# Products with the values in quarter-array tiles over two PSUM banks, probabilities scaled on ScalarE, and a new order of the attention steps

## The chip, the cores and the metric

The kernel runs on one core of a Trainium2 chip. The metric is the device time of one execution in microseconds (us), the median of several runs; less is better. The engines named below are TensorE (PE; PEld is its weight load), VectorE (DVE), ScalarE (ACT), GpSimd (POOL) and SyncE (SP).

## What is computed

The reference is one decoder layer over 512 positions of width 1024. A sliding-window attention and a Mamba-2 mixer (SSD) run side by side and are merged by gates; a gated MLP follows. The change touches only the attention, which is this:

```
qb = q.reshape(Bsz, nb, W, N_KV_HEADS, G, HEAD_DIM)
...
scores = jnp.einsum('bnqhgd,bnshd->bnhgqs', qb, kb).astype(jnp.float32) * (HEAD_DIM ** -0.5)
...
valid = (dist >= 0)[None] & (dist < WINDOW)[None] & (kpos >= 0)
...
m = jnp.maximum(scores.max(axis=-1), sink)
p = jnp.where(valid, jnp.exp(scores - m[..., None]), 0.0)
denom = p.sum(axis=-1) + jnp.exp(sink - m)
probs = (p / denom[..., None]).astype(v.dtype)
out = jnp.einsum('bnhgqs,bnshd->bnqhgd', probs, vb)
```

There are 4 blocks of 128 positions, 4 key/value heads with 4 query heads each, and head size 64. A query sees its own block up to itself, and of the block before it the keys behind its own place there: of the two triangles each fills half of a 128x128 square.

## The kernel before

Every projection is a product of float32 numbers split into a rounded part (`_hi`) and a rest (`_lo`); `three` issues three matmuls for each of 8 slices of the width. A tile of 128 output features is a **unit**: 24 matmuls of 128x512 on TensorE. Two units make a **chunk**, for which the weights are loaded (SyncE), rounded (ScalarE, `w_hi`, L576) and subtracted (VectorE, `w_lo`, L856) one chunk ahead. Chunks 3 to 6 (units 6 to 13) are the queries, 7 to 10 (units 14 to 21) `bc`, 11 and 12 `xs`, 13 and 14 `z`, 15 and 16 `xs`, 17 and 18 `z`. A unit of `bc` or `xs` also has a causal convolution: ScalarE starts `conv_acc` from the unit's bank (L772), VectorE adds three taps from the same bank (L1207), ScalarE takes tanh (L776) and VectorE makes the output (L1212). Even units use bank 0 and odd ones bank 1, so a unit can start only when VectorE has done the third tap of the unit two before it (semaphore `conv_tap`). A unit of `z` needs only a tanh and one VectorE operation.

Attention rides on these units. It has 16 **steps** n, one for each key/value head and block; `att_step(n)` gives head and block, and steps 2i and 2i+1 are a **pair**: two heads of the same block. Of the eight pairs two (steps 0 and 1, 8 and 9) are of the first block and have no block before them. A step runs through these stages:

- TensorE `scores` (for both steps of a pair, L1305 and L1311) into banks 2 to 5; ScalarE `own_scores` copies the own block (L608); VectorE `mask_and_max` masks the block before, takes the maximum and prepares the bias (L931 to L939).
- ScalarE `exponentials`, with the sums of the rows (L614, L617); VectorE `probabilities`: denominator, reciprocal and the scaling of 128x512 probabilities (L944, L946, L948).
- TensorE `probs_t` transposes four heads' probabilities into bank 6 (L1321); VectorE `probs_t_masked` copies them out under the two masks (L956, L958).
- TensorE `values`, once a pair, multiplies them by the values into bank 7 (L1331); ScalarE `attended_hi` rounds the result (L623) and VectorE `attended_lo` takes the rest (L967).

Nothing is scheduled at run time: each engine works its own list in order and waits on semaphores. The place of a stage in the lists comes from two tables. `ATT_AT[n]` is the start of step n in units, counted from unit 14, and `ATT_STAGES` adds to it a number of slots for each engine and stage. TensorE has two slots in a unit (slot 0 after its first half, slot 1 at its end). ScalarE and VectorE have three: before they start on the unit's result, after `conv_acc` or the taps, and at the end. `SSD_STAGES` does the same for the Mamba-2 steps from unit 38 on. `take(bank, semaphore, value)` makes TensorE wait for the last reader of a bank before it writes it, and notes who will read it next.

## Time and profile before

| | |
|---|---|
| Time, median of 3 runs | 1030.68 us (1030.05 to 1030.86) |
| Time of the profiled execution | 1030.5 us |
| Its span | 1028.8 us |
| TensorE busy | 1019.6 us, 99% |
| VectorE busy | 642.0 us, 62% |
| ScalarE busy | 457.5 us, 44% |
| GpSimd busy | 69.4 us, 7% |
| Granted TensorE clock | full in all slices |

The span is from the first to the last record of the trace; the execution's own time is 1.7 us longer. Busy shares are over the whole span, in which stages with different limits follow one another. Matmuls are pipelined and their records overlap, so the distance from one start to the next says more than a record's length.

### The profile page before, as it was taken

To read this page: it belongs to the slowest core of one execution; us is meant where nothing else is said; L and a number is where in the kernel's file an instruction comes from. 1 tells how busy PE (TensorE), PEld (TensorE's weight loads), DVE (VectorE), ACT (ScalarE), POOL (GpSimd) and SP (SyncE) were. 2 spreads that over 40 slices of the span, in tenths; PEclk is the share of its full clock that TensorE was granted. 3 is DMA by queue.
4 is the path that set the end of the run, shared out by engine and by line. 5 is a ranking of instruction groups with operands and counts; after the bars stand their busy time and mean duration, and the time that the engine had idled before them with its cause. 6 is when DMAs were issued, how large, how long until landed. Compare 5 with 4: busy or idle time off the path is not lost.

```text
span 1028.8 us, 13393 instructions
## 1 busy us (share of the span) xinstructions
PE 1019.6 (99%) x5095; PEld 832.2 (81%) x5095; DVE 642.0 (62%) x909; ACT 457.5 (44%) x818; POOL 69.4 (7%) x112
## 2 busy tenths in 40 slices
PE   9999999999999999999999999999999999999997
PEld 8887777777788888888888888898888888888886
DVE  7636999794476685985754544666666676641323
ACT  6344555454555545765533222544444444331233
POOL 0000000000231120122220100000000000000000
PEclk9999999999999999999999999999999999999999
DMA  7622221225556424445362743223232223332322
GB/s 219 123 85 82 83 62 63 83 83 120 159 133 162 133 72 137 140 127 153 100 205 82 266 143 108 77 82 113 91 122 82 82 85 119 93 128 87 95 69 82
DMA packets 123498, 116.48 MB, mean 113 GB/s; under 512 B 21342, under 2 KB 111782, under 8 KB 123447
## 3 DMA queue, kind: packets, MB, share of 16 engines
q1 hardware_dynamic: 95509, 94.74, 29.9%
q10 hardware_dynamic: 25346, 12.59, 5.2%
q0 software_dynamic: 2592, 8.46, 2.2%
q8 instruction: 34, 0.56, 0.2%
q14 instruction: 17, 0.14, 0.0%
HBM read 109.41 MB, written 6.36 MB: 113 GB/s over the span
## 4 chain that ended last, share of the span: by engine, by line
PE 89%; DVE 8%; ACT 2%; issue 1%; DMA 0%; SPq 0%; ACTq 0%; DVEq 0%
PE banks L1259 27%; PE banks L1260 27%; PE banks L1261 27%; DVE conv_acc L1207 3%; PE banks L1363 1%; DVE w_lo L856 1%; PE banks L1356 1%; PE banks L1331 1%; PE banks L1351 1%; PE banks L1339 1%; DMA w_raw<-in_w_in 0%; ACT probs L614 0%; PE banks L1321 0%; PE banks L1311 0%; ACT w_hi L576 0%
## 5 line engine op out<-in xcount | busy, mean ns | idle before, releaser
L856 DVE TENSOR_TENSOR w_lo<-w_raw,w_hi 128x1024 fp32r<-128x1024 f32 (+1 forms) x166 | 198.3, 1234 | 123.7 <-ACT w_hi L576 122.4
L576 ACT ACTIVATE w_hi<-w_raw 128x1024 fp32r<-128x1024 f32 (+1 forms) x166 | 164.1, 1037 | 109.2 <-PE banks L1261 107.9
L1259 PE MATMUL banks<-xn_hi,w_hi 128*128 128x512 f32 x528 | 211.5, 401 | 0.0
L1260 PE MATMUL banks<-xn_lo,w_hi 128*128 128x512 f32 x528 | 206.1, 390 | 0.0
L1261 PE MATMUL banks<-xn_hi,w_lo 128*128 128x512 f32 x528 | 206.0, 390 | 0.0
L1259 PE MATMUL banks<-hn_hi,w_hi 128*128 128x512 f32 (+1 forms) x376 | 141.3, 376 | 0.0
L1260 PE MATMUL banks<-hn_lo,w_hi 128*128 128x512 f32 (+1 forms) x376 | 141.2, 375 | 0.0
L1261 PE MATMUL banks<-hn_hi,w_lo 128*128 128x512 f32 (+1 forms) x376 | 141.2, 375 | 0.0
L1259 PEld LDWEIGHTS banks<-xn_hi,w_hi 128*128 128x128 f32 x528 | 99.1, 188 | 28.2 <-issue 8.5
L1261 PEld LDWEIGHTS banks<-xn_hi,w_lo 128*128 128x128 f32 x528 | 99.1, 188 | 21.4
L1260 PEld LDWEIGHTS banks<-xn_lo,w_hi 128*128 128x128 f32 x528 | 99.3, 188 | 19.0
L1261 PEld LDWEIGHTS banks<-hn_hi,w_lo 128*128 128x128 f32 x376 | 70.8, 188 | 12.9
L1259 PEld LDWEIGHTS banks<-hn_hi,w_hi 128*128 128x128 f32 x376 | 70.8, 188 | 12.8
L1260 PEld LDWEIGHTS banks<-hn_lo,w_hi 128*128 128x128 f32 x376 | 70.8, 188 | 12.6
L1259 PE MATMUL banks<-w_hi,act_hi 128*128 128x512 f32 x176 | 68.5, 389 | 0.0
L1260 PE MATMUL banks<-w_lo,act_hi 128*128 128x512 f32 x176 | 68.5, 389 | 0.0
L1261 PE MATMUL banks<-w_hi,act_lo 128*128 128x512 f32 x176 | 68.5, 389 | 0.0
L1207 DVE SCALAR_TENSOR_TENSOR conv_acc<-banks,half_conv,conv_acc 128x511 f32<-128x511 f32 (+2 forms) x72 | 53.8, 747 | 4.8 <-ACT conv_acc L772 3.0
L1259 PE MATMUL banks<-y_hi,w_hi 128*128 128x512 f32 x128 | 50.0, 391 | 0.0
L1261 PE MATMUL banks<-y_hi,w_lo 128*128 128x512 f32 x128 | 49.8, 389 | 0.0
L1260 PE MATMUL banks<-y_lo,w_hi 128*128 128x512 f32 x128 | 49.8, 389 | 0.0
L1028 DVE SCALAR_TENSOR_TENSOR conv_acc<-banks,param_cols,conv_acc 128x511 f32<-128x511 f32 (+1 forms) x44 | 32.9, 748 | 23.2 <-ACT conv_acc L693 20.3
(221 smaller groups left out, 1429.8 us busy)
## 6 DMA issues: line engine op xcount, KB each, us to landing
w_raw<-in_w_in SPq DMA_DIRECT2D x29, 1024.0 KB, 5.4
w_raw<-in_w_up SPq DMA_DIRECT2D x22, 1024.0 KB, 5.0
decay<-acs_scratch ACTq DMA_DIRECT2D x16, 512.0 KB, 5.9
w_raw<-in_w_ssd_o SPq DMA_DIRECT2D x8, 1024.0 KB, 5.3
w_raw<-in_w_down SPq DMA_DIRECT2D x8, 1024.0 KB, 5.0
w_raw<-in_w_in SPq DMA_DIRECT2D x16, 256.0 KB, 4.5
w_raw<-in_w_attn_o SPq DMA_DIRECT2D x16, 256.0 KB, 4.7
decay_off<-acs_scratch ACTq DMA_DIRECT2D x32, 128.0 KB, 3.6
```

What stands on the lines that cost most here:

```text
L576: A.activation(whi[:, c % 2, lo_:hi_], raw[:, c % 2, lo_:hi_], ACT.Copy).then_inc(w_rounded, 1)
L856: V.tensor_tensor(wlo[:, c % 2, lo_:hi_], raw[:, c % 2, lo_:hi_], f32(whi[:, c % 2, lo_:hi_]), ALU.subtract).then_inc(w_split, 1)
L1028: V.scalar_tensor_tensor(out=acc[:, back:SEQ], in0=PS[:, 2 * j + u, 0:SEQ - back], scalar=FW(2 - back, j, 2 * it + u), in1=acc[:, back:SEQ ...
L1207: V.scalar_tensor_tensor(out=acc[:, back:SEQ], in0=b[:, 0:SEQ - back], scalar=CW(3 - back, t), in1=acc[:, back:SEQ], op0=ALU.mult, op1=ALU ...
L1259: T.matmul(out_, w[0], m[0], start=first, stop=False)
L1260: T.matmul(out_, w[0], m[1], start=False, stop=False)
L1261: return T.matmul(out_, w[1], m[0], start=False, stop=last)
L1331: ins = T.matmul(PS[rows, 7, :], v[:, b_ - back, (g + hh) * HD:(g + hh + 1) * HD], probs.rearrange("p j q -> p (j q)"), start=back == 1 or ...
L1339: ins = T.transpose(PS[:, 2, t * P:(t + 1) * P], xs[:, TG * g + t, tok], ident[:, :])
L1351: T.matmul(PS[:, 6, :], bncb[:, 0:P], xcd[:, :], start=True, stop=True)
L1356: T.matmul(PS[:, 4, t * P:(t + 1) * P], st[:, t * P:(t + 1) * P], bc[:, NG + g, tok], start=True, stop=True)
L1363: ins = T.matmul(PS[o:o + HD, 5, (hd // 2) * P:(hd // 2 + 1) * P], xc[:, hd * HD:(hd + 1) * HD], ag[:, n % 3, hd, :], start=True, stop=True)
```

## The change

The values' products are cut into halves of keys and of queries. `part(keys, queries, back, start, stop)` issues two matmuls, one for each head of the pair, with 64 keys, 64 output features and 4 x 64 query columns. Early keys go to bank 2 and late ones to bank 7. Three quarters of each square are computed; the quarter that the mask leaves empty is skipped (in the first block it is computed once, so that bank 7 is filled). ScalarE copies bank 2 into the new tile `attended` (`attended_left`), VectorE adds bank 7 to it (`attended_sum`), and `attended_hi` and `attended_lo` read that tile and no bank. VectorE no longer scales the probabilities: its stage is now called `denominators`, and ScalarE has a stage `probabilities` with four activations of 128x128. The two tables change: transposes and values are one TensorE slot (half a unit) later in a step, and the steps from 3 on start 0.25 or 0.5 units earlier.

```diff
 ATT_STAGES = (
-    ("PE", "scores", 1), ("PE", "probs_t", 5), ("PE", "values", 7), ("ACT", "own_scores", 1),
-    ("ACT", "exponentials", 4), ("ACT", "attended_hi", 10),
-    ("DVE", "mask_and_max", 1), ("DVE", "probabilities", 4), ("DVE", "probs_t_masked", 7),
-    ("DVE", "attended_lo", 10))
+    ("PE", "scores", 1), ("PE", "probs_t", 6), ("PE", "values", 8), ("ACT", "own_scores", 1),
+    ("ACT", "exponentials", 4), ("ACT", "probabilities", 5), ("ACT", "attended_left", 11), ("ACT", "attended_hi", 12),
+    ("DVE", "mask_and_max", 1), ("DVE", "denominators", 4), ("DVE", "probs_t_masked", 8),
+    ("DVE", "attended_sum", 11), ("DVE", "attended_lo", 12))
...
-ATT_AT = (-4.5, -3.25, -2, -0.5, 1, 2.75, 4.5, 6.25, 8, 9.75, 11.5, 13, 14.25, 15.5, 16.75, 18)
+ATT_AT = (-4.5, -3.25, -2, -0.75, 0.75, 2.5, 4.25, 6, 7.75, 9.25, 11, 12.5, 13.75, 15, 16.25, 17.5)
...
+        if _n == 0 and _w == "load_decay":
+            _v = -6
...
+        att = sb("attended", [P, 2, GQ, HD], 136)
...
+                    elif what == "attended_left":
+                        if n % 2:
+                            eng.wait_ge(a_pv, n // 2 + 1)
+                            A.activation(att[:, :, :, :].rearrange("p h j q -> p (h j q)"), PS[:, 2, :],
+                                         ACT.Copy).then_inc(a_left, 1)
+                    elif what == "probabilities":
+                        eng.wait_ge(a_rd, n + 1)
+                        for j in range(GQ):
+                            ins = A.activation(Pr[:, n % 2, j, :], Pr[:, n % 2, j, :], ACT.Identity,
+                                               scale=rden[:, n % 2, j:j + 1])
+                        ins.then_inc(a_pr, 1)
...
-                        eng.wait_ge(a_pv, n // 2 + 1)
...
+                        eng.wait_ge(a_sum, n // 2 + 1)
...
-                        eng.wait_ge(a_rd, n + 1)
-                        V.tensor_tensor(Pr[:, k, :, :], Pr[:, k, :, :], bcast(rden[:, k, :], GQ, P),
-                                        ALU.mult).then_inc(a_pr, 1)
...
+                    elif what == "attended_sum":
+                        if n % 2:
+                            eng.wait_ge(a_left, n // 2 + 1)
+                            av = att[:, :, :, :].rearrange("p h j q -> p (h j q)")
+                            V.tensor_tensor(av, av, PS[:, 7, :], ALU.add).then_inc(a_sum, 1)
...
-                        take(7, a_ol, n // 2 + 1)
-                        for back in (1, 0) if b_ else (0,):
+                        take(2, a_left, n // 2 + 1)
+                        take(7, a_sum, n // 2 + 1)
+
+                        def part(keys, queries, back, start, stop):
+
                             for hh in range(2):
-                                rows = slice(hh * HD, (hh + 1) * HD)
-                                probs = ptp_of[hh][:, :, :] if back else ptc[:, hh, :, :]
-                                ins = T.matmul(PS[rows, 7, :], v[:, b_ - back, (g + hh) * HD:(g + hh + 1) * HD],
-                                               probs.rearrange("p j q -> p (j q)"), start=back == 1 or b_ == 0,
-                                               stop=back == 0)
+                                ks, qs = slice(keys * HD, keys * HD + HD), slice(queries * HD, queries * HD + HD)
+                                probs = ptp_of[hh][ks, :, qs] if back else ptc[ks, hh, :, qs]
+                                ins = T.matmul(PS[hh * HD:(hh + 1) * HD, (2, 7)[keys],
+                                                  queries * GQ * HD:(queries + 1) * GQ * HD]
+                                               .rearrange("p (j q) -> p j q", j=GQ),
+                                               v[ks, b_ - back, (g + hh) * HD:(g + hh + 1) * HD],
+                                               probs, start=start, stop=stop)
+                            return ins
+
+                        if b_:
+                            part(0, 0, 1, True, False)
+                            part(1, 1, 1, True, False)
+                            part(0, 0, 0, False, True)
+                            part(1, 1, 0, False, True)
+                            part(0, 1, 0, True, True)
+                            ins = part(1, 0, 1, True, True)
+                        else:
+                            part(0, 0, 0, True, True)
+                            part(1, 1, 0, True, True)
+                            part(0, 1, 0, True, True)
+                            ins = part(1, 0, 0, True, True)
```

What these tables move is seen in the engines' lists. Line numbers of the changed kernel differ: L1259 to L1261 are now L1277 to L1279, L1331 is L1352, L576 is L580, L772 is L787, L776 is L791.

**TensorE**, near unit 30. `probs_t_prev` with two numbers is the block before for the two heads of the pair, `v` the values. Before:

```order
L1261 MATMUL banks<-xn_hi,w_lo 128x512
L1331 MATMUL banks<-probs_t_prev_86,v 64x512
L1331 MATMUL banks<-probs_t_prev_87,v 64x512
L1331 MATMUL banks<-probs_t_cur,v 64x512 x2
L1321 MATMUL banks<-ident,probs 128x128 x4
```

And in the changed kernel, for the values of steps 10 and 11:

```order
L1279 MATMUL banks<-xn_hi,w_lo 128x512
L1352 MATMUL banks<-probs_t_prev_87,v 64x256
L1352 MATMUL banks<-probs_t_prev_88,v 64x256
L1352 MATMUL banks<-probs_t_prev_87,v 64x256
L1352 MATMUL banks<-probs_t_prev_88,v 64x256
L1352 MATMUL banks<-probs_t_cur,v 64x256 x6
L1352 MATMUL banks<-probs_t_prev_87,v 64x256
L1352 MATMUL banks<-probs_t_prev_88,v 64x256
L1339 MATMUL banks<-ident,probs 128x128 x4
L1329 MATMUL banks<-kT,qT 64x192 x16
```

Four matmuls with 512 columns have become twelve with 256, and the scores of steps 14 and 15, which write bank 2 again, now stand in the same place behind values and transposes.

**ScalarE**, from the tanh of unit 19 to the tanh of unit 20. `w_hi` is the rounding of the weights of chunk 11. Before:

```order
L776 ACTIVATE conv_tanh<-conv_acc 128x512
L614 ACTIVATE probs,small<-scores,small 128x128 x4
L617 ACTIVATE small<-small 128x4
L576 ACTIVATE w_hi<-w_raw 128x1024 x2
L623 ACTIVATE a_hi<-banks 128x4x128
L772 ACTIVATE conv_acc<-banks,half_conv 128x512
L608 ACTIVATE scores<-banks 128x512
L776 ACTIVATE conv_tanh<-conv_acc 128x512
```

And in the changed kernel:

```order
L791 ACTIVATE conv_tanh<-conv_acc 128x512
L630 ACTIVATE probs<-probs,small 128x128 x4
L580 ACTIVATE w_hi<-w_raw 128x1024 x2
L625 ACTIVATE attended<-banks 128x512
L787 ACTIVATE conv_acc<-banks,half_conv 128x512
L638 ACTIVATE a_hi<-attended 128x2x4x64
L612 ACTIVATE scores<-banks 128x512
L791 ACTIVATE conv_tanh<-conv_acc 128x512
```

The exponentials of step 6 moved ahead of the tanh of unit 19, and the scaling of its probabilities stands between that tanh and the rounding of the weights; the copy of bank 2 stands ahead of `conv_acc` of unit 20.

**VectorE**, from the outputs of unit 21 (`bc`) to those of unit 22 (`xs`). `small` holds denominators and maxima, `neg_tile` marks step 8, which is of the first block. Before:

```order
L944 TENSOR_TENSOR small<-small 128x4
L946 RECIPROCAL small<-small 128x4
L948 TENSOR_TENSOR probs<-probs,small 128x512
L1212 SCALAR_TENSOR_TENSOR bc<-conv_tanh,conv_acc 128x512
L856 TENSOR_TENSOR w_lo<-w_raw,w_hi 128x1024 x2
L1207 SCALAR_TENSOR_TENSOR conv_acc<-banks,half_conv,conv_acc 128x511
L1207 SCALAR_TENSOR_TENSOR conv_acc<-banks,half_conv,conv_acc 128x510
L1207 SCALAR_TENSOR_TENSOR conv_acc<-banks,half_conv,conv_acc 128x509
L956 TENSOR_TENSOR probs_t_prev_87<-banks,mask_prev_t 128x512
L958 TENSOR_TENSOR probs_t_cur<-banks,tri 128x512
L931 COPY_PREDICATED scores<-mask_prev,neg_tile 128x512
```

And in the changed kernel:

```order
L959 TENSOR_TENSOR small<-small 128x4
L961 RECIPROCAL small<-small 128x4
L1230 SCALAR_TENSOR_TENSOR bc<-conv_tanh,conv_acc 128x512
L871 TENSOR_TENSOR w_lo<-w_raw,w_hi 128x1024 x2
L946 COPY_PREDICATED scores<-mask_prev,neg_tile 128x512
L949 TENSOR_REDUCE small<-scores 128x4
L951 TENSOR_TENSOR small<-small 128x4
L953 TENSOR_SCALAR small<-small 128x4
L954 TENSOR_TENSOR small<-small 128x4
L1225 SCALAR_TENSOR_TENSOR conv_acc<-banks,half_conv,conv_acc 128x511
L1225 SCALAR_TENSOR_TENSOR conv_acc<-banks,half_conv,conv_acc 128x510
L1225 SCALAR_TENSOR_TENSOR conv_acc<-banks,half_conv,conv_acc 128x509
```

The scaling is gone, and the block of the maximum of step 8, which stood behind the taps of unit 22, stands ahead of them.

## Rows read from the trace of the kernel before

**Rows 1.** Busy time by stage, 115 to 180 us; columns: stretch, its length, engines.
```profile
115.00:180.00 65.00, 64.21 (x368) 49.08 (x368) 58.84 (x103) 35.52 (x90) 0.00 (x0) 1.00 0.21 66
```

**Rows 2.** Chain of waits; columns: start us, length us, what.
```profile
121.03 1.53 ACT probs L614 x8
123.17 0.69 DVE probs L948
```

**Rows 3.** Timeline of TensorE around the values of the third pair.
```profile
131.31 0.39 PE L1261 MATMUL banks<-xn_hi,w_lo 128*128 128x512 f32 x1
131.63 1.08 PE L1331 MATMUL banks<-probs_t_prev,v 128*64 128x512 f32 x4
...
133.50 0.50 PE L1259 MATMUL banks<-xn_hi,w_hi 128*128 128x512 f32 x1
```

**Rows 4.** Timeline of TensorE around scores with two blocks of keys.
```profile
124.50 1.53 PE L1311 MATMUL banks<-kT,qT 64*64 64x192 f32 x32
125.96 0.50 PE L1259 MATMUL banks<-xn_hi,w_hi 128*128 128x512 f32 x1
```

**Rows 5.** Timeline of TensorE at two waits for VectorE.
```profile
147.51 0.39 PE L1261 MATMUL banks<-xn_hi,w_lo 128*128 128x512 f32 x1
148.27 0.66 PE L1321 MATMUL banks<-ident,probs 128*128 128x128 f32 x4 [0.37 <-DVE probs L948]
148.86 1.10 PE L1311 MATMUL banks<-kT,qT 64*64 64x64 f32 x32
149.89 0.50 PE L1259 MATMUL banks<-xn_hi,w_hi 128*128 128x512 f32 x1
...
179.00 0.39 PE L1261 MATMUL banks<-xn_hi,w_lo 128*128 128x512 f32 x1
179.81 1.08 PE L1331 MATMUL banks<-probs_t_cur,v 128*64 128x512 f32 x4 [0.42 <-DVE probs_t_cur L958]
180.82 0.50 PE L1259 MATMUL banks<-xn_hi,w_hi 128*128 128x512 f32 x1
```

**Rows 6.** Timeline of VectorE; in brackets idle time before the row.
```profile
116.14 2.32 DVE L1207 SCALAR_TENSOR_TENSOR conv_acc<-banks,half_conv,conv_acc 128x511 f32<-128x511 f32 x3
...
127.39 0.73 DVE L931 COPY_PREDICATED scores<-mask_prev,banks 128x512 f32<-128x512 int32 x1
...
129.23 0.68 DVE L956 TENSOR_TENSOR probs_t_prev<-banks,mask_prev_t 128x512 f32<-128x512 f32 x1
...
130.43 2.31 DVE L1207 SCALAR_TENSOR_TENSOR conv_acc<-banks,half_conv,conv_acc 128x511 f32<-128x511 f32 x3
...
135.14 0.16 DVE L944 TENSOR_TENSOR small<-small 128x4 f32<-128x4 f32 x1 [1.01 <-ACT small L617]
...
147.13 0.15 DVE L944 TENSOR_TENSOR small<-small 128x4 f32<-128x4 f32 x1
...
147.53 0.69 DVE L948 TENSOR_TENSOR probs<-probs,small 128x512 f32<-128x512 f32 x1
148.14 0.68 DVE L1212 SCALAR_TENSOR_TENSOR bc<-conv_tanh,conv_acc 128x512 f32<-128x512 f32 x1
148.86 2.36 DVE L856 TENSOR_TENSOR w_lo<-w_raw,w_hi 128x1024 fp32r<-128x1024 f32 x2
151.13 2.31 DVE L1207 SCALAR_TENSOR_TENSOR conv_acc<-banks,half_conv,conv_acc 128x511 f32<-128x511 f32 x3
```

**Rows 7.** Timeline of ScalarE, in attention and behind it.
```profile
147.24 0.63 ACT L776 ACTIVATE conv_tanh<-conv_acc 128x512 f32<-128x512 f32 x1 [2.34 <-DVE conv_acc L1207]
147.78 1.99 ACT L576 ACTIVATE w_hi<-w_raw 128x1024 fp32r<-128x1024 f32 x2
149.68 0.76 ACT L772 ACTIVATE conv_acc<-banks,half_conv 128x512 f32<-128x512 f32 x1
...
245.86 1.28 ACT L645 ACTIVATE decay<-decay,small 128x128 f32<-128x128 f32 x4
250.76 0.60 ACT L783 ACTIVATE conv_tanh<-banks 128x512 f32<-128x512 f32 x1 [3.62 <-PE banks L1261]
```

12 lines of the change are left out of this document (7 added, 5 removed).

## The prediction, made before the changed kernel ran

> **What bounds the kernel now.** I read the stages first. Attention runs from 60 to 240 us of the span, beside the projections. In its middle, 115 to 180 us, TensorE is busy for 64.21 of 65 us and VectorE for 58.84; ScalarE has 35.52 [rows 1]. So TensorE bounds the time, with VectorE just behind it. The chain of waits agrees: there it runs over ScalarE's exponentials and VectorE's scaling, and not over TensorE [rows 2]. Away from this stretch it runs nearly everywhere over TensorE. What shortens TensorE's own work shortens the kernel, if VectorE delivers.
>
> I call a tile of projections (24 matmuls) a unit. From the second half of unit 20 (133.50) to the last matmul of unit 22 (147.51) lie 59 matmul steps, one group of transposes (0.44) and 0.10 after the values [rows 3, 5]: 13.47 / 59 = 0.228 us a step, 5.48 us a unit.
>
> **TensorE's work.** Now the values of a pair of heads take 131.63 to 133.50, 1.87 us: eight records of 128*64 tiles, two heads side by side, each product in two passes [rows 3]. A pass streams 512 columns; four in a row make about 1.71 us and 0.16 stays for start and end. The first block has no keys before it: 1.01 us (179.81 to 180.82) [rows 5].
>
> No row shows the new form, 64*64 tiles with 256 columns. The nearest are the scores, which run in such tiles with different banks for the two row halves, exactly as here: 32 passes of 192 columns take 1.46 us (124.50 to 125.96), and 32 of which half have 128 and half 64 take 1.03 (148.86 to 149.89) [rows 4, 5]. With a pass at 512 columns worth 0.427, 192 columns are 0.160, and 32 passes over four tiles 1.28: 0.18 is left. For the second, the tiles with 128 columns need 8 x 0.107 = 0.85, and again 0.18 is left. So four tiles overlap fully, and the longest one counts. The new form has 24 passes of 0.213: 6 x 0.213 + 0.18 = 1.46 us. First block: 4 x 0.213 + 0.18 = 1.03. Six pairs have a block before them, two have none: 6 x (1.46 - 1.87) + 2 x 0.02 = **-2.4 us**. Bounds: the two rows above leave hardly 0.1 a pair (0.6 in all); without any overlap of the row halves it is a rival below.
>
> **Waits that go.** TensorE waits for VectorE's scaling before the transposes at 148.27: the gap from 147.51 is 0.76 instead of 0.23. It waits for masked probabilities at 179.81: 0.81 instead of the 0.32 that rows 3 show [rows 3, 5]. Transposes half a unit (2.7 us) later, and the masking of that pair now ahead of the rounding of weights on VectorE, take both away: 0.53 + 0.49 = **-1.0 us**. Bounds: 0 and -1.2 (there is a smaller wait of this kind near 124 us).
>
> **What VectorE and ScalarE get.** VectorE loses 16 scalings, which hold it for 0.61 each (147.53 to 148.14) and gains 8 sums, priced by the same form at 0.6 [rows 6]: 16 x 0.61 - 8 x 0.6 = 5 us less. ScalarE gains 16 groups of four scalings. The nearest row is the decay's activation of 128x128 with a column operand: four in 1.28 us [rows 7]; the next instruction can start after about 1.2. It also gains 8 copies out of a bank, at most 0.6 each. That is 24 us more on an engine with much idle time. As a sum this costs nothing; as an order it does, since both sit in a loop: VectorE's taps, ScalarE's tanh, what is queued behind it, then the weights' rounding or the next unit's start, then VectorE again.
>
> The Trainium skill, TensorEngine Tiling (Array Packing), Performance Considerations, speaks against this change: tiling speeds up TensorE but not the reading of its banks, and the copy may become the bottleneck. By it the second bank's copy and sum would eat the gain; the sum below finds that the copy costs little and ScalarE's scalings the most. No row here decides it.
>
> **The new wait.** I follow VectorE from the taps of unit 17, which start at 116.14 [rows 6] and which nothing ahead moves by more than some 0.2, to the taps of unit 22, which free the bank for unit 24. Prices as the distance to the next row where they overlap: taps 2.23 (2.31 busy, of which 0.08 overlaps), output 0.60, block of maximum 1.84, masking 1.20, denominators 0.40, rounding rest of two half chunks 2.27 [rows 6]. The changed order has there 6 taps (13.4), 3 maskings (3.6), 5 outputs (3.0), 3 denominators (1.2), 3 roundings (6.8), 3 blocks of maximum (5.5; now there are two, the third stands behind these taps), one sum and one rest of attention (1.2): 34.7 us.
>
> VectorE's idle time for ScalarE is added, with tanh 0.54, w_hi 1.90 (half of it 0.95), conv_acc 0.7 [rows 7], exponentials 1.63 (rows 2 show 1.53 for the chain's part):
> - unit 17: tanh and exponentials (2.2) against masking and output (1.8): 0.4; then the first half of w_hi against the denominators: 0.55
> - unit 18: w_hi, the scaling and conv_acc (1.9 + 1.2 + 0.7 = 3.8) against 3.2 of VectorE: 0.6
> - units 19 and 21: after the taps ScalarE does tanh, now the scaling, then half of w_hi (0.6 + 1.2 + 1.0 = 2.8), VectorE only denominators and output (1.0): 1.8, twice.
>
> That is 5.2 us. Today the longest one there is 1.01 [rows 6]. With 0.4 of small gaps the taps of unit 22 end at 116.14 + 34.7 + 5.2 + 0.4 = 156.4.
>
> TensorE arrives at unit 24 as follows. Unit 22 ends today at 147.51 + 0.23 = 147.74, without its wait. Two values before it save 0.82, a wait 0.17, and the scores that stand behind unit 22 now stand inside it (+1.23 with their gaps): 147.9. Unit 23 with its transposes adds 5.92: 153.8. So TensorE waits 156.4 - 153.8 = **+2.6 us**. The pair's values stand behind this point now and ahead of it before, so nothing of the wait is made good there. In the next units VectorE has spare time again (a TensorE stop gives it that), and the z units, in which it has no taps to do, have room.
>
> **Small terms.** In unit 30 the changed order puts values, transposes and scores in one place, and the scores want bank 2, which ScalarE copies out only after the values: 0.1 to start, 0.6 for the copy, minus 0.4 of transposes between: **+0.3**. Four places in place of three have scores right behind transposes, which costs 0.05 each, and one place fewer has values before them: **+0.1**. The load of the first decay goes behind two roundings of weights: its four activations, now at 245.86, start some 2 us later, into the 3.62 us in which ScalarE idles before 250.76 [rows 7]; cost nothing, up to 1 us if that idle time were gone. The new `take(2, ...)` ahead of the values waits for a maximum block that is a unit older; nothing. No queue of SyncE or GpSimd moves.
>
> **Sum.** -2.4 - 1.0 + 2.6 + 0.3 + 0.1 = -0.4 on the profiled execution's 1030.5, which is 0.2 under the median of the runs: 1030.1 by the one, 1030.3 by the other. The wait of 2.6 is the softest term, and a TensorE unit that comes a little late shortens it: I shade it to 2.3, **1030.0 us**. A change within 0.2% (2.1 us, about what a measurement of this kernel can tell from none) is the likeliest, 1028.6 to 1032.7.
>
> **Rivals.**
> 1. The wait at unit 24 doesn't come, because VectorE, 5 us lighter, reaches unit 17 early or ScalarE's scalings fall into its idle time: -2.4 - 1.0 + 0.4 = 1027.5 to the median's scale. For it: ScalarE is busy only 55% of the stretch [rows 1]. Against it: the two scalings of units 19 and 21 stand exactly where VectorE has nothing else. Half of the wait gives 1028.8, so the wait must be under 1.2 us to pass the bound. Chance 0.38 for faster by over 0.2%.
> 2. Slower: the loop binds in each of the five unit pairs from 14 to 24, and not in two. Each pair adds 1.2 to 1.8 of idle time (the scaling ahead of w_hi); three more make 3.6 to 5.4, and VectorE's lag grows by that less what it saves (2 us). Then the waits are 2.6 + 2 to 3.4 and the time 1032 to 1033.5. It decides from a total wait of 5 us on. Chance 0.13.
> 3. The change doesn't do what it says: the row halves don't run side by side. Then 24 passes over two tiles take 12 x 0.213 + 0.18 = 2.74 us, +0.87 for six pairs and +0.86 for two, 7 us more work, of which the wait at unit 24 hides some: 1034 to 1037. The scores' rows are against it. Chance 0.04.
>
> **Range.** Forecast 0.45, faster 0.38, slower 0.17. From rival 1's full gain to the start of rival 2's loss: 1027.4 to 1032.5. Own range of the forecast: 1028.7 to 1031.5.
>
> **What would show it.** Values at 1.4 to 1.5 us from first matmul to the next projection, in four-tile form; over 1.7 would sink the first term. No wait before the transposes near 147 or the values near 179. A gap before the first projection of unit 24, near 154, released by VectorE's taps (`conv_acc`), with `w_lo` starting over 1 us after the output before it, and w_hi behind a scaling on ScalarE. A gap of 0.3 before scores near 205. If TensorE's gap near 154 is missing, the prediction is wrong on the fast side; if such gaps stand before several units, on the slow side. No difference is expected after 245 us.

## The result, and the profile after

The median of 20 runs is 1032.57 us (1030.43 to 1034.8); the kernel before has 1030.53 (1030.03 to 1031.35, 20 runs). The ratio is 1.0019, 95% interval 1.0013 to 1.0025: slower by about 0.2%. I had forecast 1030.0 and a range to 1032.5, which the median just misses. The difference is small but clear of the noise, and it goes the other way than I forecast. Two things in these numbers need explaining. The profiled execution is one of the quick ones, 1030.94 us, 1.6 us below the median of its own kernel. And the runs lie 4.4 us apart, those of before 1.3.

The profiled execution first. The values' products in the changed kernel's timeline of TensorE (start, length, engine, line, operation, tiles, count; in brackets the idle time ahead and its releaser):

```profile
133.26 0.39 PE L1279 MATMUL banks<-xn_hi,w_lo 128*128 128x512 f32 x1
133.58 0.66 PE L1352 MATMUL banks<-probs_t_prev,v 64*64 64x256 f32 x8
...
134.72 0.38 PE L1352 MATMUL banks<-probs_t_prev,v 64*64 64x256 f32 x2
135.04 0.50 PE L1277 MATMUL banks<-xn_hi,w_hi 128*128 128x512 f32 x1
```

From 133.58 to 135.04 are 1.46 us, where [rows 3] had 1.87. Four tiles run side by side, as the first term had it. The waits at the transposes near 147 and the values near 179 [rows 5] are gone; the waits of TensorE between 150 and 240 us are one row (waited for in all, times, longest):

```profile
PE banks L1277 <- DVE conv_acc L1225: 3.4, 2, 2.7
```

The two are these. At unit 24, on TensorE:

```profile
153.76 0.39 PE L1279 MATMUL banks<-xn_hi,w_lo 128*128 128x512 f32 x1
156.87 0.50 PE L1277 MATMUL banks<-xn_hi,w_hi 128*128 128x512 f32 x1 [2.72 <-DVE conv_acc L1225]
```

The step is 3.11 us in place of 0.23, a stop of 2.88. How VectorE came to be late is seen two units earlier, first ScalarE and then VectorE:

```profile
133.11 0.63 ACT L791 ACTIVATE conv_tanh<-conv_acc 128x512 f32<-128x512 f32 x1 [2.34 <-DVE conv_acc L1225]
133.65 1.26 ACT L630 ACTIVATE probs<-probs,small 128x128 f32<-128x128 f32 x4
134.82 2.00 ACT L580 ACTIVATE w_hi<-w_raw 128x1024 fp32r<-128x1024 f32 x2
```

```profile
133.78 0.69 DVE L1230 SCALAR_TENSOR_TENSOR bc<-conv_tanh,conv_acc 128x512 f32<-128x512 f32 x1 [0.42 <-ACT conv_tanh L791]
135.89 2.36 DVE L871 TENSOR_TENSOR w_lo<-w_raw,w_hi 128x1024 fp32r<-128x1024 f32 x2 [1.43 <-ACT w_hi L580]
```

The scaling stands between tanh and `w_hi` for 1.17 us, and VectorE, with nothing else to do, waits 1.43. The same happens at 150.36.

The second wait, at unit 34, is in no term of the sum:

```profile
231.58 0.60 PE L1339 MATMUL banks<-ident,probs 128*128 128x128 f32 x4
232.83 0.50 PE L1277 MATMUL banks<-xn_hi,w_hi 128*128 128x512 f32 x1 [0.65 <-DVE conv_acc L1225]
```

TensorE goes on 1.25 us after transposes that take 0.35 from their start to the next one's (231.62 to 231.97 in the kernel before): 0.9 lost. ScalarE and then VectorE before it:

```profile
227.65 0.62 ACT L638 ACTIVATE a_hi<-attended 128x512 fp32r<-128x512 f32 x1
228.47 1.28 ACT L630 ACTIVATE probs<-probs,small 128x128 f32<-128x128 f32 x4 [0.20 <-DVE small L961]
229.66 0.77 ACT L787 ACTIVATE conv_acc<-banks,half_conv 128x512 f32<-128x512 f32 x1
```

```profile
228.35 0.66 DVE L984 TENSOR_TENSOR a_lo<-attended,a_hi 128x512 fp32r<-128x512 f32 x1
230.46 2.32 DVE L1225 SCALAR_TENSOR_TENSOR conv_acc<-banks,half_conv,conv_acc 128x511 f32<-128x511 f32 x3 [1.44 <-ACT conv_acc L787]
```

Here the scaling stands ahead of `conv_acc`, and VectorE's taps wait for that. The stretches, to be read beside [rows 1] (length, then busy time and instructions of PE, PEld, DVE, ACT, POOL, the granted clock, DMA share, GB/s):

```profile
115.00:180.00 65.00, 62.28 (x393) 48.60 (x392) 56.12 (x100) 42.02 (x111) 0.00 (x0) 1.00 0.21 66
180.00:240.00 60.00, 59.22 (x384) 45.84 (x382) 45.81 (x85) 36.85 (x103) 0.00 (x0) 1.00 0.25 77
```

TensorE was idle for 0.79 us of the first stretch and is for 2.72 now, with both other engines far from full: two engines wait for each other in turn, and neither is the bound by its load.

To compare executions I use TensorE's own marks, from the row of a line's matmuls (count, least/median/longest ns, first and last start): the first projection with `xn_hi` and the first with `a_hi`. Between them lies all of the attention. Before, and after:

```profile
L1259 PE MATMUL banks<-xn_hi,w_hi x528: 389/389/504, 26.3 to 526.4; 128*128 128x512 f32 x176
L1259 PE MATMUL banks<-a_hi,w_hi x64: 389/389/504, 262.2 to 363.2; 128*128 128x512 f32 x64
```

```profile
L1277 PE MATMUL banks<-xn_hi,w_hi x528: 389/389/504, 26.2 to 526.9; 128*128 128x512 f32 x176
L1277 PE MATMUL banks<-a_hi,w_hi x64: 389/389/504, 262.7 to 363.7; 128*128 128x512 f32 x64
```

I call the distance of the first starts the attention stretch: 235.9 us before, 236.5 after. It leaves out what differs from run to run at the start (the mark itself lies between 25.5 and 27.3 us in the 15 traces of the study) and later on. From the first `y_hi` matmul (528.4 in this trace) to the last of the gated MLP every trace has 494.1 or 494.2 us.

### The profile page after: what moved, and what is told of

It is laid out like the page before. It is cut to its first block, busy times and chain, and to the rows that moved or that the text cites. A ratio compares the mean times of both kernels' runs of the same rounds, so it can differ in the third digit from the quotient of the medians.

```text
span 1029.2 us, 13697 instructions
## 1 busy us (share of the span) xinstructions
PE 1017.7 (99%) x5215; PEld 835.0 (81%) x5215; DVE 636.1 (62%) x901; ACT 480.4 (47%) x890; POOL 70.1 (7%) x112
## 4 chain that ended last, share of the span: by engine, by line
PE 91%; DVE 6%; ACT 2%; issue 1%; DMA 0%; SPq 0%; ACTq 0%; DVEq 0%
PE banks L1277 28%; PE banks L1279 27%; PE banks L1278 27%; DVE conv_acc L1225 2%; PE banks L1400 1%; DVE w_lo L871 1%; PE banks L1393 1%; PE banks L1388 1%; PE banks L1352 1%; PE banks L1329 1%; PE banks L1376 1%; DMA w_raw<-in_w_in 0%; PE banks L1339 0%; ACT probs L630 0%; PE banks L1288 0%
## 5 line engine op out<-in xcount | busy, mean ns | idle before, releaser
L1277 PE MATMUL banks<-xn_hi,w_hi 128*128 128x512 f32 x528 | 211.7, 401 | 3.4 <-DVE conv_acc L1225 3.4
L580 ACT ACTIVATE w_hi<-w_raw 128x1024 fp32r<-128x1024 f32 (+1 forms) x166 | 164.1, 1037 | 107.6 <-PE banks L1279 107.6
L1279 PE MATMUL banks<-xn_hi,w_lo 128*128 128x512 f32 x528 | 206.0, 390 | 0.0
L1277 PE MATMUL banks<-hn_hi,w_hi 128*128 128x512 f32 (+1 forms) x376 | 141.3, 376 | 0.0
L1279 PE MATMUL banks<-hn_hi,w_lo 128*128 128x512 f32 (+1 forms) x376 | 141.2, 375 | 0.0
L1277 PEld LDWEIGHTS banks<-xn_hi,w_hi 128*128 128x128 f32 x528 | 99.2, 188 | 29.9 <-issue 6.1
L1279 PEld LDWEIGHTS banks<-xn_hi,w_lo 128*128 128x128 f32 x528 | 99.1, 188 | 21.5
L1279 PEld LDWEIGHTS banks<-hn_hi,w_lo 128*128 128x128 f32 x376 | 70.8, 188 | 12.8
L1277 PEld LDWEIGHTS banks<-hn_hi,w_hi 128*128 128x128 f32 x376 | 70.8, 188 | 12.6
L1277 PE MATMUL banks<-w_hi,act_hi 128*128 128x512 f32 x176 | 68.5, 389 | 0.0
L1279 PE MATMUL banks<-w_hi,act_lo 128*128 128x512 f32 x176 | 68.5, 389 | 0.0
L1277 PE MATMUL banks<-y_hi,w_hi 128*128 128x512 f32 x128 | 50.0, 391 | 0.0
L1279 PE MATMUL banks<-y_hi,w_lo 128*128 128x512 f32 x128 | 49.8, 389 | 0.0
```

The costliest lines, as they stand in the source:

```text
L580: A.activation(whi[:, c % 2, lo_:hi_], raw[:, c % 2, lo_:hi_], ACT.Copy).then_inc(w_rounded, 1)
L1277: T.matmul(out_, w[0], m[0], start=first, stop=False)
L1279: return T.matmul(out_, w[1], m[0], start=False, stop=last)
```

## The experiments

Theory A: the stop of nearly 3 us at unit 24 also makes TensorE's granted clock fall in many executions, and that lifts the median over the profiled one. Theory B: the spread has another source. Beside them stands the question of which part of the change makes the wait. Two further theories came up during the study, both on why runs of a kernel differ: theory C, the new form of the values makes them differ; theory D, only a wait at unit 24 does. Medians are of the kernel named; the kernel before had 1030.25 to 1030.56 beside them. Each row is explained below.

| kernel | attention stretch | profiled | median (lowest to highest) |
|---|---|---|---|
| before | 235.9 | 1030.5 | 1030.53 (1030.03 to 1031.35) |
| changed | 236.5 | 1030.94 | 1032.57 (1030.43 to 1034.8) |
| changed again | 236.4 | 1030.48 | 1032.68 (1030.48 to 1033.7) |
| changed, two single executions | 238.0, 238.0 | 1035.27, 1032.63 | |
| step 8's maximum behind the taps | 235.3 | 1029.44 | 1030.24 (1029.44 to 1031.51) |
| scaling on VectorE | 234.0 | 1028.96 | 1029.55 (1028.22 to 1031.22) |
| scaling behind the rounding | 234.8 | 1029.35 | 1029.89 (1028.54 to 1031.69) |
| both places | 234.3 | 1030.17 | 1029.95 (1028.19 to 1031.2) |
| all but the scaling, maximum behind | 233.0 | 1026.74 | 1027.0 (1026.74 to 1028.55) |
| order alone | 234.7 | 1028.8 | 1028.8 (1028.62 to 1029.76) |
| order and scaling | 236.4 | 1031.55 | 1031.09 (1030.34 to 1031.59) |
| before, new values alone | 238.9 | 1033.83 | 1033.7 (1032.94 to 1036.15) |
| before, one stop of 3 us | 239.9 | 1034.49 | 1034.3 (1033.37 to 1035.53) |
| before, stops at z | 240.0 | 1044.6 | 1044.35 (1043.89 to 1044.88) |

### The changed kernel again, three times

> The changed kernel as it is, once more, for a second profiled execution. Theory A (TensorE's granted clock falls after the long stop at unit 24 in most executions): if the profiled one is among the longer runs, 1032 us or more, the stretch right behind the stop, 157 to 162 us, shows matmul steps of 0.43 in place of 0.227 us and a granted clock of about 0.5, worth 1.5 to 3 us, and no other place differs. If it is a quick one near 1030.9 the clock is full there as in the first. Theory B: a long run shows full clock there and the time is lost in several other waits. Median 1032 to 1033 by both.

> The changed kernel again, one profiled execution, to have one of its longer executions (over 1032 us) in a trace. Theory A: behind the stop at unit 24, from 157 us on, matmul steps of 0.43 us and a granted clock near 0.5 for 3 to 5 us. Theory B: full clock there, the time lost in other places.

> As the run before it, a further profiled execution of the changed kernel; the same is expected of it.

The repeat gave a median of 1032.68 and again a quick profiled execution, 1030.48. The two single executions were long ones, 1035.27 and 1032.63. The second of them, TensorE's timeline and windows:

```profile
153.84 0.39 PE L1279 MATMUL banks<-xn_hi,w_lo 128*128 128x512 f32 x1
157.01 0.75 PE L1277 MATMUL banks<-xn_hi,w_hi 128*128 128x512 f32 x1 [2.78 <-DVE conv_acc L1225]
157.56 0.63 PE L1278 MATMUL banks<-xn_lo,w_hi 128*128 128x512 f32 x1
157.98 0.63 PE L1279 MATMUL banks<-xn_hi,w_lo 128*128 128x512 f32 x1
```

```profile
153.80:156.80 3.00, 0.43 (x2) 0.01 (x1) 2.86 (x7) 0.00 (x0) 0.00 (x0) 1.00 0.96 304
157.00:160.00 3.00, 2.99 (x7) 2.41 (x8) 2.19 (x6) 3.00 (x12) 0.00 (x0) 0.51 0.06 20
160.00:164.00 4.00, 4.00 (x34) 2.60 (x34) 3.83 (x8) 3.11 (x8) 0.00 (x0) 0.94 0.00 0
```

The quick execution of the changed kernel, the same window behind the stop:

```profile
157.00:160.00 3.00, 3.00 (x16) 2.23 (x20) 2.32 (x6) 3.00 (x12) 0.00 (x0) 1.00 0.09 27
```

The same stop stands in all four traces (3.11, 3.12, 3.11 and 3.17 from start to start). In two of them the steps behind it are 0.43 us in place of 0.227: half the clock, 1.2 in place of 2.4 GHz, 7 matmul records in place of 16 in three microseconds. Both executions have an attention stretch of 238.0, 1.5 us longer. Of 32 runs of the changed kernel 18 have a mean granted clock of 0.997 or less over the whole program, and their median is 1032.9; the other 14 have 0.998 to 1.0 and 1031.1. (The mean is a rough mark: it takes in the end of the program, where the clock halves too, and the 1035.27 execution has 0.998 although its clock did fall behind the stop. So 18 is rather a lower bound.) Of 80 runs of the kernel before that were taken beside the experiments none has less than 0.998, and none of the 79 runs of the eight kernels below in which TensorE never stops for over 2 us. That a fall follows the stop, and costs 1.5 us, is shown in two traces; that it happens in somewhat over half of the runs is argued from the means, which give 1.8 us between the two groups.

The traces say something on why it comes in one execution and not in the next. In all 15 the clock also falls at the end of the program, where TensorE has nothing more to do. In windows of 0.1 us, the fall lies from 2.4 us (the run with stops at z) to 5.1 us (the order alone) behind the start of the last matmul; the four traces of the changed kernel have 3.4, 3.2, 4.8 and 2.9. So the delay differs from one execution to the next. Behind the last matmul ahead of unit 24 it was 3.4 and 3.3 us in the two long executions, when TensorE had just gone on after 3.1 and 3.2; the two quick ones went on after 3.1 and had no fall. A stop of this length lies within the scatter of the delay.

The first single execution is longer by 2.6 us than the second. Its start is 0.9 later (27.3 against 26.4). It has also waits of ScalarE that the quick execution has not, between 400 and 460 us:

```profile
ACT decay_off L683 <- DMA decay_off<-acs_scratch: 1.7, 1, 1.7
```

A transfer of the Mamba-2 part lands late, and TensorE loses 1.7 us between `a_hi` and `y_hi` (267.4 against 265.7). So B has a share as well: start and late transfers, 2.6 us between these two executions, in which the wait and the fall are the same.

### Step 8's maximum behind the taps of unit 22

```diff
-ATT_AT = (..., 6, 7.75, 9.25, ...)
+ATT_AT = (..., 6, 8, 9.25, ...)
```

> The changed kernel, with step 8's block of maximum (1.86 us on VectorE) behind the taps of unit 22 again and no more ahead of them. In the changed kernel's trace these taps end at 156.8 and TensorE is there at 153.8. Without the block they end near 155.0, so the wait at unit 24 falls from 2.88 to about 1.1 us; the smaller one at unit 34 stays. Theory A (a wait near 3 us on TensorE also makes its granted clock fall for a few microseconds in many executions, and this is what lifts the median of 1032.57 over the profiled execution of 1030.94): the wait gives 1.8 us and the lower clock goes with it, median 1028.8 to 1029.5, runs within 1.5 us of each other. Theory B (the spread of the runs comes from something else in the new order, such as ScalarE's load or the loop of the rounded weights): only the 1.8 us go, median 1030.3 to 1031, the runs still spread over 3 us or more.

The edit puts every stage of step 8 one slot later, on all three engines; the block of the maximum is what leaves VectorE's list ahead of the taps. TensorE at unit 24:

```profile
153.43 0.39 PE L1279 MATMUL banks<-xn_hi,w_lo 128*128 128x512 f32 x1
154.74 0.50 PE L1277 MATMUL banks<-xn_hi,w_hi 128*128 128x512 f32 x1 [0.92 <-DVE conv_acc L1225]
```

The step is 1.31, a wait of 1.08, as expected. The block now delays the masking behind it, and the next values wait 0.60 for that (`PE banks L1352 <- DVE probs_t_cur L970`), so that 1.2 of the 1.8 us are kept. None of 11 runs has a mean clock under 0.998, and the median falls by 2.3, more than the stretch alone, which speaks for A. But A's own forecast missed: 1030.24 is over its 1028.8 to 1029.5 (0.6 of that is the wait before the values) and close to B's 1030.3, and the spread of 2.1 us is not down to 1.5. The median is also 0.8 above the profiled execution, with no fall of the clock in any run; so part of the 1.6 us between the two in the changed kernel has another source than the clock.

### The kernel before, with one stop of 3 us

```diff
                         k_conv += 1
                         take(b, c_tap, 3 * k_conv)
+                        if k_conv == 11:
+                            eng.wait_ge(a_rd, 9)
```

> The kernel before with one wait added: TensorE starts unit 24 only when VectorE has the reciprocals of step 8 (160.46 in its trace), where it now starts at 157.42. All else is as before. It is a stop of TensorE of about 3.0 us, as long as the one that the change makes, without the change. Theory A (the stop also lowers the granted clock in many executions): the time rises by 3 us and by 1 to 2 more in the median, 1034.5 to 1035.5, runs spread over 3 us or more, and the longer runs show the lower mean clock. Theory B: it rises by the stop alone, 1033.0 to 1033.6, with the spread of before, about 1.3 us.

Nothing of the change is in this kernel, and the clock falls here too:

```profile
155.00:160.00 5.00, 2.47 (x11) 0.67 (x9) 4.83 (x11) 3.26 (x12) 0.00 (x0) 1.00 0.15 52
160.90:163.50 2.60, 2.60 (x8) 2.02 (x7) 2.60 (x4) 1.73 (x3) 0.00 (x0) 0.50 0.00 0
163.90:170.00 6.10, 6.10 (x31) 5.01 (x30) 3.15 (x7) 0.78 (x1) 0.00 (x0) 1.00 0.57 175
```

The stretch grows by 4.0 us: 2.9 of stop (156.44 to 160.32, less the 0.95 that the values take there) and 1.6 at half speed (8 steps of 0.43), less the 0.49 wait at the first block's values [rows 5], which is gone because the stop lets VectorE catch up. The median is 3.7 over before (expected 4 to 5 by A, 2.5 to 3 by B), and 4 of 6 runs have 0.997 or less. They spread over 2.2 us, not the 3 expected by A. The stop alone makes the clock fall; the change is needed for it only as the maker of the stop.

### The kernel before, with stops at the units of z

```diff
                         take(b, z_out, k_z)
+                        if k_z > 1:
+                            eng.wait_ge(z_tanh, k_z - 1)
```

> The kernel before with several short stops of TensorE in place of one long one: each unit of z starts only when ScalarE has done the tanh of the unit of z before it, 0.1 + 0.63 us after that unit's end. That is six places (units 27 to 29 and 35 to 37), two or three of them partly covered by scores or transposes: 3 to 4.5 us of idle TensorE in all, none longer than 1 us. Theory A: short stops cost what they last and the granted clock stays full: the time rises by the sum of the gaps, 1033.5 to 1035, and the runs agree within 1.5 us. The rival (it is the amount of idle time in the stretch, not one long stop): as in the kernel with one stop of 3 us, the clock falls behind some of them, 1 to 3 us more and a spread of 3 us.

The median rose by 14 us, not by 3 to 4.5: I had counted 8 units of z, and there are 16; and at one of them ScalarE is far behind. The run still says what it was made for. Windows with two short stops (1.17 and 1.12 us from start to start) inside, then around the one long one (4.47), and behind it; and TensorE's waits:

```profile
172.00:188.00 16.00, 14.49 (x89) 10.33 (x82) 11.08 (x22) 8.82 (x19) 0.00 (x0) 1.00 0.21 67
396.00:402.00 6.00, 2.14 (x10) 1.44 (x8) 3.17 (x5) 5.87 (x7) 0.00 (x0) 0.89 0.28 76
402.20:407.40 5.20, 5.18 (x12) 4.12 (x13) 0.59 (x1) 0.00 (x0) 0.00 (x0) 0.50 0.67 216
```

```profile
PE banks L1259 <- ACT conv_tanh L783: 8.6, 6, 4.1
PE banks L1259 <- issue: 1.8, 3, 0.7
```

The clock stays full behind the short stops and is halved for over 5 us behind the long one. Waits of 10.4 and 2.6 lost at half speed are 13.0 of the 14.1 us by which this execution is longer; the rest I did not trace. The other three runs have mean clocks of 0.998 and the same times, 1043.89 to 1044.88: whether the clock fell in them too stays open.

### The scaling back on VectorE

```diff
-("ACT", "probabilities", 5)
...
                         V.reciprocal(rden[:, k, :], den[:, k, :]).then_inc(a_rd, 1)
+                        eng.wait_ge(a_rd, n + 1)
+                        V.tensor_tensor(Pr[:, k, :, :], Pr[:, k, :, :], bcast(rden[:, k, :], GQ, P),
+                                        ALU.mult).then_inc(a_pr, 1)
```

> The changed kernel with the scaling of the probabilities back on VectorE (one operation of 0.61 us behind the reciprocals) and none on ScalarE; new tables, products with the values and copy of bank 2 stay. Up to the taps of unit 22 VectorE gets three scalings more (1.8 us) and waits less for ScalarE: 1.2 less in units 19 and 21 each, 0.6 in unit 18, 3.0 in all. The wait at unit 24 falls from 2.88 to about 1.7 us, and the one at unit 34 goes (0.8). My prediction's account (ScalarE's scaling ahead of the rounding of weights makes most of VectorE's idle time, and so most of the wait): the profiled execution near 1029.0, and VectorE's idle of 1.43 before w_lo in units 19 and 21 down to about 0.3. The rival (it is the load of VectorE that makes the wait): VectorE later than in the changed kernel, the wait at 24 3.5 us or more, 1031.5 and more. Under theory A (clock falls after a long stop) the median lies close to the profiled execution in the first case.

VectorE has more to do and is earlier. The step at unit 24:

```profile
153.94 0.39 PE L1276 MATMUL banks<-xn_hi,w_lo 128*128 128x512 f32 x1
155.44 0.50 PE L1274 MATMUL banks<-xn_hi,w_hi 128*128 128x512 f32 x1 [1.11 <-DVE conv_acc L1222]
```

1.50 in place of 3.11, and at unit 34 0.76 in place of 1.25: 2.1 us, and the stretch falls by 2.5. `w_lo` at 135.65 and 148.94 starts without any wait that the timeline would show. My account holds, and the rival (VectorE's load) falls; the wait became shorter than I expected (1.27 over the natural step, not 1.7).

### The scaling on ScalarE, behind the rounding of weights

```diff
+        if (_e, _w) == ("ACT", "probabilities") and _s % 6 == 5:
+            _s += 1
```

> The changed kernel with ScalarE's scaling moved behind the rounding of weights wherever it stood right ahead of it; the same work, in another order on ScalarE alone. My account of the wait at unit 24 (the scaling of 1.17 us stands between the tanh and w_hi in units 19 and 21, and VectorE, which has nothing else then, waits for w_hi): VectorE's two idle times of 1.43 us fall to about 0.3, the taps of unit 22 end near 154.5, the wait falls from 2.88 to 0.4 to 0.9 us, profiled 1028.6 to 1029.2, median within 0.6 of that. The rival (ScalarE's load as such holds the loop, wherever the scaling stands; the idle time only moves to another operation): the wait stays above 2 us and the time above 1030.3.

The same work in another order. VectorE:

```profile
133.06 0.69 DVE L1233 SCALAR_TENSOR_TENSOR bc<-conv_tanh,conv_acc 128x512 f32<-128x512 f32 x1 [0.41 <-ACT conv_tanh L794]
134.01 2.36 DVE L874 TENSOR_TENSOR w_lo<-w_raw,w_hi 128x1024 fp32r<-128x1024 f32 x2 [0.25 <-ACT w_hi L583]
```

1.43 became 0.25, twice. The step at unit 24 is 1.68 (152.84 to 154.52), a wait of 1.45 where I expected 0.4 to 0.9: of the 2.4 us that the two places give, VectorE passes on 1.4, since small waits for `conv_acc` (0.31) and the own scores (0.23) take their place. The stretch falls by 1.7. The profiled 1029.35 is a little over the 1028.6 to 1029.2 expected. So the position costs about half of this wait (1.4 of 2.9), and here the load costs something too.

### The parts alone

New values alone, in the order of before, with the scaling on VectorE:

```diff
-("ACT", "attended_hi", 10), ... ("DVE", "attended_lo", 10)
+("ACT", "attended_left", 10), ("ACT", "attended_hi", 11), ... ("DVE", "attended_sum", 10), ("DVE", "attended_lo", 11)
```

> The kernel before with one part of the change: the values' products in quarter-array tiles over banks 2 and 7, with ScalarE's copy, VectorE's sum, and the rounding from the sum. Scaling on VectorE and the order of before stay (the rounding of attention comes a slot later, the load of the first decay too). By the prediction's term: six pairs at 1.46 in place of 1.87 us and two at 1.03, 2.4 us less of TensorE's work. VectorE has 8 sums of 0.6 more; its wait at 148.27 may grow by that (0 to 0.6). Expected 1028.0 to 1028.7 with the spread of before. The rival (the second bank's copy and sum hold TensorE up elsewhere, above all the scores that want bank 2): a wait of 0.5 us or more before scores in several places, and 1029.5 to 1031.

It is 3 us slower where I had expected it about 2 us quicker, by a wait that I had put at 0 to 0.6 us and at one place. TensorE's waits from 115 to 240 us, of this kernel:

```profile
PE banks L1336 <- DVE probs L957: 5.1, 4, 1.7
PE banks L1349 <- DVE probs_t_cur L967: 0.6, 1, 0.6
```

and VectorE ahead of the first of them:

```profile
113.94 0.68 DVE L973 TENSOR_TENSOR attended<-attended,banks 128x512 f32<-128x512 f32 x1
115.31 0.69 DVE L981 TENSOR_TENSOR a_lo<-attended,a_hi 128x512 fp32r<-128x512 f32 x1 [0.70 <-ACT a_hi L632]
```

A pair costs VectorE 1.3 us here and not 0.6: the sum, and a wait for ScalarE's rounding of it, since sum, rounding and rest follow one another at once. In an order in which the transposes wait for VectorE's scaling already [rows 5], that comes out on TensorE at four places before transposes and one before values: from start to start they lose 5.4 us more than before, less the 2.4 of the values, and the stretch is 3.0 longer. The Trainium skill's page TensorEngine Tiling (Array Packing), Performance Considerations, was cited in the prediction for this (emptying the banks may become the bottleneck); in this order the trace agrees.

The new order alone, with the old values and the scaling on VectorE:

```diff
-("PE", "probs_t", 5), ("PE", "values", 7) ... ("DVE", "probs_t_masked", 7)
+("PE", "probs_t", 6), ("PE", "values", 8) ... ("DVE", "probs_t_masked", 8)
...
-ATT_AT = (-4.5, -3.25, -2, -0.5, 1, 2.75, ...)
+ATT_AT = (-4.5, -3.25, -2, -0.75, 0.75, 2.5, ...)
```

> The kernel before with the new order alone: transposes and values half a unit later, steps from 3 on 0.25 or 0.5 units earlier, the masked copies a slot later on VectorE, and the rounding of attention too. Values in their old form (1.87 us), scaling on VectorE, no second bank. The waits before the transposes at 148.27 and the values at 179.81 go: 1.0 us. With the products in the new form and the scaling on VectorE the wait at unit 24 was 1.1 us; here VectorE has no sum (0.6 less) and TensorE arrives 0.8 later (two values), so it is 0 to 0.3. Expected 1029.4 to 1029.9 by my account. The rival (the order by itself makes the wait at unit 24, whatever the rest): 1.5 us or more of wait there and 1031 or more.

The ratio is 0.9986 (0.9977 to 0.9995), and 1028.8 is below the 1029.4 to 1029.9 expected. TensorE has no wait at all between 115 and 240 us, and the stretch is 234.7, 1.2 less. The order does not make the wait.

The order and the scaling on ScalarE, with the old values:

```diff
-("DVE", "probabilities", 4)
+("ACT", "probabilities", 5), ("DVE", "denominators", 4)
```

> The new order with the scaling on ScalarE, and the values in their old form: the change without its first part. Against the run with the order alone the taps of unit 22 come later by what the scaling on VectorE saved in the changed kernel, 2.73 - 1.11 = 1.6 us. There was no wait at unit 24 in that run; I expect 0.8 to 1.4 us now and 0.4 at unit 34, 1029.8 to 1030.6 by my account. By the rival (without the sum VectorE has the room, the scaling on ScalarE costs nothing): 1028.8. On the spread: theory C (the new form of the values makes runs differ) expects 1.3 us or less; theory D (the wait at unit 24 does) more, if the wait is over 1 us.

The steps are 1.30 at unit 24 and 0.85 at unit 34: waits of 1.07 and 0.5, in the bounds expected, and the stretch is 1.7 longer than with the order alone. The time of 1031.09 is half a microsecond over what I gave. With the new order, the scaling on ScalarE brings the wait without the new values. These make it longer by 1.8 us: counted from the first projection, TensorE comes to unit 24 0.7 earlier and VectorE's taps end 1.1 later (0.6 of it the sum). So the new values, with the scaling on ScalarE, gain nothing: the stretch is 236.4 without them and 236.5 with them.

### Without the wait

The changed kernel with the scaling on VectorE and step 8's maximum behind the taps, the edits of two runs above together:

> The changed kernel with both causes of the wait at unit 24 taken away: the scaling on VectorE, and step 8's block of maximum behind the taps of unit 22. In the run with the scaling on VectorE alone the wait was 1.11 us; the block is 1.86, so it goes. Left are the new form of the values (2.4 us less) and the new order (the waits of 1.0 us gone), with 0.3 to 0.4 before the scores near 204 and as much at unit 34. Expected 1027.5 to 1028.2, the quickest so far. On the spread: the kernels with the new form of the values have so far spread over 2 to 4 us, those without it (before, and the order alone) over 1.2. Theory C (the new form of the values itself makes runs differ): 2 us or more here too. Theory D (runs differ only where TensorE waits for VectorE at unit 24 for more than about 1 us): within 1.3 us, as no such wait is left.

1027.0 us, ratio 0.9970 (0.9957 to 0.9982), quicker than both kernels and than the 1027.5 to 1028.2 expected. TensorE's waits that are left between 115 and 240 us:

```profile
PE banks L1349 <- DVE probs_t_cur L967: 0.2, 1, 0.2
PE banks L1274 <- DVE conv_acc L1222: 0.2, 1, 0.2
```

```profile
115.00:180.00 65.00, 64.80 (x415) 50.63 (x414) 62.64 (x112) 38.40 (x96) 0.00 (x0) 1.00 0.23 72
```

VectorE is busy for 62.64 of 65 us, more than in any kernel here, and TensorE for 64.80. The new values are in, and five of six runs lie within 0.32 us, the sixth 1.5 above: a spread of 1.8, between the 1.3 that theory D expects and the 2 or more of theory C (the new values make runs differ). Six runs don't decide it. The table speaks rather for C: the six kernels with the new values and no long stop spread over 1.8 to 3.2 us, the two with the old ones and no long stop over 1.1 and 1.3, as the kernel before. How the new values would do that no run shows.

All three parts, with both places set:

```diff
-ATT_AT = (..., 6, 7.75, 9.25, ...)
+ATT_AT = (..., 6, 8, 9.25, ...)
...
+        if (_e, _w) == ("ACT", "probabilities") and _s % 6 == 5:
+            _s += 1
```

> The changed kernel with all its parts, and two stages placed otherwise: ScalarE's scaling behind the rounding of weights where it stood ahead of it, and step 8's block of maximum behind the taps of unit 22. With the first alone the step at unit 24 was 1.68 us where 0.23 is natural; the block is 1.86, so the wait goes. If the waits and what the clock loses behind the long one are the whole of the difference, the profiled execution is 1029.35 - 1.45 + 0.2 (the wait before the next values, as in the kernel with the scaling on VectorE) = 1028.1, and the runs show no mean clock under 0.998; against the kernel with the scaling on VectorE (1026.7) it has 0.5 more at unit 34. If ScalarE's scaling costs by itself, a wait of 1 us or more is left in units 17 to 26 and the time stays above 1029.

No wait is left at unit 24, and no run has a mean clock under 0.998. But the stretch is 234.3 against 233.0 with the scaling on VectorE: TensorE waits 0.5 before values, 0.2 before transposes and 0.9 at unit 34 (0.6 in its row of waits). The two places explain 2.2 of the 3.5 us by which the changed kernel's stretch exceeds the shortest one; 1.3 is left to the scaling on ScalarE, of which 0.5 is a matter of place again: at unit 34 it still stands ahead of `conv_acc` (0.9 lost in place of 0.4). The profiled execution missed my 1028.1 by 2.1: its start is 0.8 later than in the run from which I had reckoned, late transfers take 0.5 more, and the stretch fell by 0.5 where I had 1.25. Its runs spread over 3 us without any wait at unit 24, so theory D (runs differ only by that wait) falls.

## Why the prediction was wrong

- **Values, -2.4**: right. 1.46 and 1.03 us in the traces, and from the order alone to the order with new values and the maximum behind the taps the stretch falls by 1.7, near the 1.5 that 2.4 less 0.3 at unit 30, 0.4 at unit 34 and 0.2 before values would make.
- **Waits that go, -1.0**: right. The order alone gives 1.2.
- **The new wait, +2.6, shaded to 2.3**: its place, its releaser and its makers were right; it measured 2.88. VectorE's idle time for ScalarE, 5.2 us by the sum, is 5.24 in the rows; what was missing is that the taps of unit 17 start 0.38 later than taken (116.52). Shading it was wrong: 0.6 lacks in the forecast by it.
- **The step that failed** is the pricing of this wait by its length. A stop of TensorE of that length costs another 1.5 us in the executions in which the granted clock falls behind it, and by the mean clocks these are at least 18 of 32. The forecast of 1030.0 is to be set against 1031.1, the median of the runs whose mean clock shows no fall; against all runs the forecast lacks 2.6. Of this, 1.1 stand against the runs without a fall and come from the shaded wait (0.6) and the one at unit 34 (0.9); the other 1.5 are the clock. Without the clock the change would have been no gain either: its sign hangs on the two waits, its size on the clock.
- **"The z units have room"**: wrong. At unit 34 the scaling stands ahead of `conv_acc` of unit 32 and costs TensorE 0.9. I had followed VectorE from unit 17 to unit 24 only, and the changed order puts scalings before `conv_acc` later on too. This is the second step that failed, a term that the sum has at nothing.
- **Unit 30, +0.3**: right, 0.79 from the transposes to the scores. Load of the decay, 0: right; the order alone has it as well and loses nothing behind 262 us.
- On the quick execution the terms as measured are -2.4 - 1.0 + 2.88 + 0.9 + 0.3 + 0.1 = +0.8, and the stretch shows +0.6.
- **Rival 1** (no wait, 1027.5; from the median, as it says, its own terms give 1027.7) did not come in this kernel; it is what the best variant became by two edits, at 1027.0. **Rival 2**'s size came about (1032 to 1033.5) by another mechanism than its own: not a loop that binds in every pair, but one stop and what the clock does behind it.

What stays open: what sets the delay with which the clock falls, and so why a stop of 3.1 us brings it in one execution and not in the next; why the kernels with the new values spread wider; and what delays the transfers of the Mamba-2 part in some executions.

## What to carry to other kernels

An activation moved to an idle engine is free only if nobody waits for what is queued behind it: here 1.2 us ahead of a rounding of weights cost the other engine 1.2 (a wait of 1.43 in place of 0.25), twice, and the engine that is busy for 96% of the stretch was the better place. A stop of the engine that bounds the time is priced in two parts, its length and what its clock loses behind it, and one profiled execution may show only the first: the spread of the runs is to be read beside it. And a change of several parts is worth taking apart: two of these three, with one step placed otherwise, gain 3 us (ratio 0.9970), and the third added to them takes it all back (1.0001).

## What the runs showed of the hardware

TensorE's granted clock fell from 2.4 to 1.2 GHz behind stops of 2.9 us (in two of four traces of the changed kernel, and in the one trace of the kernel before with a stop put in) and in the one of about 4.2, and stayed full in the traces behind every stop of 1.0 to 1.8 us. Behind the last matmul of the program it fell in all 15 traces, after 2.4 to 5.1 us. After a stop it was at full speed again 3.4 to 3.7 us after TensorE went on, and 5.3 us after the stop of 4.2. The Trainium skill, TensorE: Matmul & The Clock Gate, Part 1, says that the clock is gated by how busy the engine has been of late, with these two levels; the traces agree, and the prediction had not weighed this page. Four 64x64 tiles with 256 columns each did overlap: 24 records took 1.46 us from the first start to the next projection, the sum of six passes of 0.213 one after another and 0.18 for start and end, by the prediction's working.
